# A hybrid decoder layer on one core: the key batches and the sample softmax moved between projection units, the memory pages turned one by one in one bank

## What is computed

```python
x = x + 0.5 * swiglu_ffn(x, ffn1_norm, ffn1_w_in, ffn1_w_out)
proj = rmsnorm(x, mix_norm) @ w_in          # u | q | k | v | q_mem, 256+512+512+512+256 columns
y_pool = pool_mixer(u, buf, ...)            # windows 2, 4, 8, 16, then 64x64 maps
q = rotary(rmsnorm(q)); k = rotary(rmsnorm(k))
y_moba = moba_attention(q, k_all, v_all)    # 8 heads; sample: 1024 cached keys in pages, best 3 of 4 blocks + own
y_mem = mem_attention(rmsnorm(qm), mk, mv)  # 4 heads into 256 memory tokens
x = x + concat(y_pool, y_moba, y_mem) @ w_out
x = x + 0.5 * swiglu_ffn(x, ffn2_norm, ffn2_w_in, ffn2_w_out)
```

## Time and profile before

| | us |
|---|---|
| three runs | 593.26, 593.95, 594.25 |
| median | 593.95 |
| the profiled execution | 594.11 |
| its span, first to last instruction | 592.3 |
| TensorE busy | 570.4 |
| VectorE busy | 394.4 |
| ScalarE busy | 264.4 |
| mean granted clock of TensorE | 0.993 |

### The profile page before, as it was taken

The page is one execution under the profiler, slowest core; times in us unless marked ns, Lnnn a source line. Parts: engine busy times, 40 slices in busy tenths (PEclk is TensorE's granted clock), DMA queues, the critical chain, the costliest instruction groups (busy, mean ns, idle before and its releaser), DMA issues.

```text
span 592.3 us, 13485 instructions
## 1 busy us (share of the span) xinstructions
PE 570.4 (96%) x5104; PEld 522.7 (88%) x5104; DVE 394.4 (67%) x707; ACT 264.4 (45%) x420; POOL 16.1 (3%) x24
## 2 busy tenths in 40 slices
PE   9999999999999999988899968999999999999997
PEld 7999999999899997655576746989999999999997
DVE  4776767768688876996654443488777776774443
ACT  5834345354543345433354654564343434353331
POOL 1000000000000003000000000040000000000000
PEclk9999999999999999998999989999999999999999
DMA  8799988775677638897999925446666666575522
GB/s 220 215 261 296 257 260 239 221 228 191 224 237 240 224 107 293 312 386 269 328 330 308 352 72 182 117 127 185 179 177 177 177 177 177 177 242 184 177 71 74
DMA packets 133121, 128.41 MB, mean 217 GB/s; under 512 B 6624, under 2 KB 103991, under 8 KB 133071
## 3 DMA queue, kind: packets, MB, share of 16 engines
q1 hardware_dynamic: 132791, 127.76, 68.5%
q10 hardware_dynamic: 288, 0.08, 0.1%
HBM read 125.12 MB, written 2.83 MB: 216 GB/s over the span
## 4 chain that ended last, share of the span: by engine, by line
PE 75%; DVE 11%; issue 5%; ACT 5%; DMA 2%; SPq 1%; DVEq 0%; ACTq 0%
PE banks L1451 21%; PE banks L1453 20%; PE banks L1452 20%; PE banks L1459 4%; DVE w_lo L976 3%; ACT w_hi L679 3%; PE banks L1860 2%; DVE kv L987 2%; PE banks L1590 2%; DMA raw<-in_w_in 1%; PE banks L1781 1%; PE banks L1560 1%; DVE h_tmp L1022 1%; DVE h_tmp L1017 1%; DVE sg L1012 1%
## 5 line engine op out<-in xcount | busy, mean ns | idle before, releaser
L976 DVE TENSOR_TENSOR w_lo<-raw,w_hi 128x1024 fp32r<-128x1024 f32 x158 | 193.3, 1230 | 107.7 <-ACT w_hi L679 106.3
L1451 PE MATMUL banks<-x_hi,w_hi 128*128 128x264 f32 x768 | 221.4, 288 | 2.5 <-DVE h_tmp L1017 0.9
L1452 PE MATMUL banks<-x_lo,w_hi 128*128 128x264 f32 x768 | 218.0, 284 | 0.0
L1453 PE MATMUL banks<-x_hi,w_lo 128*128 128x264 f32 x768 | 217.9, 284 | 0.0
L679 ACT ACTIVATE w_hi<-raw 128x1024 fp32r<-128x1024 f32 x158 | 161.8, 1050 | 89.3 <-PE banks L1453 76.0
L1451 PEld LDWEIGHTS banks<-x_hi,w_hi 128*128 128x128 f32 x768 | 145.0, 189 | 5.8 <-issue 2.2
L1452 PEld LDWEIGHTS banks<-x_lo,w_hi 128*128 128x128 f32 x768 | 145.2, 189 | 0.0
L1453 PEld LDWEIGHTS banks<-x_hi,w_lo 128*128 128x128 f32 x768 | 144.4, 188 | 0.0
L1451 PE MATMUL banks<-h_hi,w_hi 128*128 (+1 forms) x352 | 100.2, 285 | 0.0
L1453 PE MATMUL banks<-h_hi,w_lo 128*128 (+1 forms) x352 | 100.2, 285 | 0.0
L1452 PE MATMUL banks<-h_lo,w_hi 128*128 (+1 forms) x352 | 100.0, 284 | 0.0
(11 more groups left out here) (280 smaller groups left out, 505.4 us busy)
## 6 DMA issues: line engine op xcount, KB each, us to landing
raw<-in_ffn_w_in SPq DMA_DIRECT2D x86, 512.0 KB, 4.3
raw<-in_ffn_w_out SPq DMA_DIRECT2D x44, 512.0 KB, 3.4
kv<-in_cache_k SPq DMA_DIRECT2D x56, 256.0 KB, 4.8
kv<-in_cache_v SPq DMA_DIRECT2D x48, 256.0 KB, 5.0
raw<-in_w_in SPq DMA_DIRECT2D x12, 512.0 KB, 6.3
late_slot<-in_cache_v SPq DMA_DIRECT2D x16, 256.0 KB, 4.6
raw<-in_w_out SPq DMA_DIRECT2D x8, 512.0 KB, 5.8
raw<-in_mem_w_kv SPq DMA_DIRECT2D x4, 512.0 KB, 3.3
```

Source lines behind the costliest of these rows:

```text
L976: vec.tensor_tensor(w_lo[:, n % RING, :], raw[:, n % RING, :], w_hi[:, n % RING, :].bitcast(F32), ALU.subtract).then_inc(lo_ready, 1)
L1451: pe.matmul(out, lhs[0], rhs[0], start=start, stop=False)
L1452: pe.matmul(out, lhs[0], rhs[1], start=False, stop=False)
L1453: return pe.matmul(out, lhs[1], rhs[0], start=False, stop=stop)
```

## The change

- The table: sample projections 4 to 7 stand together ahead of unit 3's last piece; key batches 0 to 4 one piece later, batches 5, 6, 7 ahead of piece 2 of unit 5, piece 2 of unit 7 and piece 3 of unit 8 (before: 0 of 5, 1 of 6, 2 of 7). The softmax steps A0 to A5 move from units 8 to 10 to units 8 to 12, value batch 0 from the end of unit 10 into unit 12, all heads a unit or more later. Pages 0 to 3 are turned during unit 15, pages 4 to 7 in the tail between other steps, each alone.
- One bank (6) and one semaphore pair for all page turns. Page 0 waits until the outputs of heads 0 to 3 have left the bank, each further page until the one before has been copied back. The scores of the last two heads wait for all pages and for pooling's banks.
- The first unit of the second feed-forward makes the products with the high part of x first, waiting for that, and those with the low part behind.
- The last four projection units take their weight blocks in the order 1, 2, 3, 0 instead of 2, 3, 0, 1; SyncE reads the page numbers of batch 6 ahead of the memory keys and those of batch 7 behind value batch 5.

```diff
-HY_BANKS, POOL_BANKS, MK_BANKS, QM_BANK = (6, 3, 4), (4, 5), (6, 5, 4), 7
+HY_BANKS, POOL_BANKS, MK_BANK, QM_BANK = (6, 3, 4), (4, 5), 6, 7
...
-J_ORDER = (2, 3, 0, 1)
+J_ORDER = (2, 3, 0, 1) * 3 + (1, 2, 3, 0)
...
-            8: {0: [("OWN", 0), ("A", 0)], 1: [("OWN", 1)], 2: [("S", 10), ("NV", 4), ("ND", 4)], 3: [("A", 1)], 4: [("A", 2), ("S", 11), ("ES", 2)]},
-            9: {0: [("A", 3), ("WL", 11)], 2: [("NS", 4), ("NG", 4), ("A", 4)], 4: [("WL", 12)]},
...
+            8: {0: [("OWN", 0)], 2: [("NV", 4), ("ND", 4)], 3: [("K", 7)], 4: [("S", 10), ("A", 0), ("OWN", 1)]},
+            9: {0: [("WL", 11)], 1: [("A", 1)], 2: [("A", 2), ("S", 11), ("ES", 2)], 4: [("WL", 12)]},
...
+            keep_pages(6)
             load_memory("mk")
-            keep_pages(6)
+            load_batch("v", 5)
             keep_pages(7)
-            load_batch("v", 5)
...
-                act.wait_ge(k_turned[b % 3], b // 3 + 1)
-                act.activation(mem_page(b), bank[MK_BANKS[b % 3]][:, :], ACT.Copy).then_inc(kT_ready[b % 3], 1)
+                act.wait_ge(k_turned, b + 1)
+                act.activation(mem_page(b), bank[MK_BANK][:, :], ACT.Copy).then_inc(kT_ready, 1)
...
-                for idx, k in enumerate((range(KT), M_ORDER)[f]):
-                    if k_at is not None:
+                order = (range(KT), M_ORDER)[f]
+                if k_at is not None:
+                    w = lambda k: weights(n % RING, k * P, (k + 1) * P)
+                    out = bank[b0 + j][:, 0:N]
+                    for idx, k in enumerate(order):
+                        pe.wait_ge(xhi_ready, k_at + idx + 1)
+                        pe.matmul(out, w(k)[0], x_hi[:, k, :], start=(idx == 0), stop=False)
+                        pe.matmul(out, w(k)[1], x_hi[:, k, :], start=False, stop=False)
+                    for idx, k in enumerate(order):
                         pe.wait_ge(xlo_ready, k_at + idx + 1)
+                        mm = pe.matmul(out, w(k)[0], x_lo[:, k, :], start=False, stop=(idx == KT - 1))
...
                 if b == 0:
                     pe.wait_ge(hy_lo, 1)
-                elif b < 3:
-                    pe.wait_ge(pool_lo, 2)
                 else:
-                    pe.wait_ge(kT_ready[b % 3], b // 3)
+                    pe.wait_ge(kT_ready, b)
...
                     if k == 5:
-                        pe.wait_ge(kT_ready[0], mem_last(6))
-                        pe.wait_ge(kT_ready[1], mem_last(5))
+                        pe.wait_ge(kT_ready, NS)
+                        pe.wait_ge(pool_lo, 2)
```

More of the change, by code:

```diff
@@ L272, in layer @@
         s_stats, s_shared, s_sums = sem("s_stats"), sem("s_shared"), sem("s_sums")
-        k_turned, kT_ready = [sem(f"k_turned{i}") for i in range(3)], [sem(f"kT_ready{i}") for i in range(3)]
+        k_turned, kT_ready = sem("k_turned"), sem("kT_ready")
         q_turned, mk_used = sem("q_turned"), sem("mk_used")
@@ L346, in mem_page @@
             return slots[SLOT_OF["mk", 0]][:, b * 512:(b + 1) * 512]
-        def mem_last(bank_):
-            return len([b for b in range(NS) if MK_BANKS[b % 3] == bank_])
         def key_pair(g):
@@ L557, in load_projection @@
             def load_projection(r):
-                j = J_ORDER[r % 4]
+                j = J_ORDER[r]
                 if r < 12:
@@ L979, in key_evac @@
             def key_evac(b):
-                vec.wait_ge(k_turned[b % 3], b // 3 + 1)
-                vec.tensor_copy(mem_page(b), bank[MK_BANKS[b % 3]][:, :]).then_inc(kT_ready[b % 3], 1)
+                vec.wait_ge(k_turned, b + 1)
+                vec.tensor_copy(mem_page(b), bank[MK_BANK][:, :]).then_inc(kT_ready, 1)
             def turn_pair(g):
@@ L1464, in ffn_unit @@
                 pe.wait_ge(lo_ready, i * 4 + (n + 1))
-                for idx, k in enumerate((range(KT), M_ORDER)[f]):
-                    if k_at is not None:
+                order = (range(KT), M_ORDER)[f]
[7 more added lines that the diff above has]
+                    for idx, k in enumerate(order):
                         pe.wait_ge(xlo_ready, k_at + idx + 1)
+                        mm = pe.matmul(out, w(k)[0], x_lo[:, k, :], start=False, stop=(idx == KT - 1))
+                for idx, k in enumerate(order if k_at is None else ()):
                     mm = three(bank[b0 + j][:, 0:N], weights(n % RING, k * P, (k + 1) * P),
@@ L1559, in project_samples @@
                         c0 = kk * 512 + q * P
-                        mm = pe.matmul(bank[S_BANK][32 * q:32 * q + NS, 0:P], xs[:, 2 * J_ORDER[j] + kk, :], raw[:, n % RING, c0:c0 + P],
+                        mm = pe.matmul(bank[S_BANK][32 * q:32 * q + NS, 0:P], xs[:, 2 * J_ORDER[r] + kk, :], raw[:, n % RING, c0:c0 + P],
                                        start=(j + kk == 0), stop=(j + kk == 4))
@@ L1568, in key_turns @@
                     pe.wait_ge(hy_lo, 1)
-                elif b < 3:
-                    pe.wait_ge(pool_lo, 2)
                 else:
-                    pe.wait_ge(kT_ready[b % 3], b // 3)
+                    pe.wait_ge(kT_ready, b)
                 for c in range(4):
-                    mm = turn(bank[MK_BANKS[b % 3]][:, c * P:(c + 1) * P], mem_page(b)[:, c * P:(c + 1) * P])
-                mm.then_inc(k_turned[b % 3], 1)
+                    mm = turn(bank[MK_BANK][:, c * P:(c + 1) * P], mem_page(b)[:, c * P:(c + 1) * P])
+                mm.then_inc(k_turned, 1)
             def key_logits(b):
@@ L1597, in mem_key_logits @@
                 pe.wait_ge(qkT_ready, 6)
-                for side in range(3):
-                    pe.wait_ge(kT_ready[side], mem_last(MK_BANKS[side]))
+                pe.wait_ge(kT_ready, NS)
                 for b in range(4):
@@ L1801, in _ @@
                     elif k == 4:
[L1802 removed]
+                        pe.wait_ge(pool_lo, 1)
                     masked = k < MH // 2
@@ L1873, in _ @@
                 pe.wait_ge(res_ready, KT + j + 1)
-                ffn_unit(1, 0, j, 2 * KT)
+                ffn_unit(1, 0, j, None if j else 2 * KT)
             ffn_unit(1, 0, 2)
```

9 lines of the change are left out of this document (3 added, 6 removed), and 44 rows, old and new, of tables (EXTRA, TAIL).

## The result

The changed kernel takes 605.27 us (median of four runs, 602.87 to 606.01); the kernel before, beside it, 593.61. The ratio is 1.019, with a 95% interval of 1.016 to 1.022. The prediction said 602.1 with a range of 597 to 607. As a difference it said 8.2 us more than before; 11.7 were measured (the interval is 9.4 to 13.1), so the time lies in the range, but nearer to rival three (605.9) than to the forecast. The profiled execution took 605.17 us with a span of 603.4, 11.1 more than before.

A forecast was written before the change was run, and what follows sets the result against it. Bound: softmax steps on in-order ScalarE held behind weight splits waiting for SyncE's full queue. 7.4 - 8.7 + 3.6 + 1.7 + 3.4 + 0.5 = 7.9, plus 0.3, on 594.1, less 0.15: 602.1 us, range 597 to 607.

The forecast's parts named there:

- rival three: Slower still: two more half-clock stretches and the upper end of the queue's delay, 605.9 us; chance 0.16.
- unit 8's weights sent: SyncE's queue: this send waits for sample projection 4 and goes out at 244.5, 2.4 us later than before.
- unit 13's weights later by: SyncE's queue: these weights land 1.5 us later, ends 0.3 and 2.4, at 290.0.
- sum A4: Softmax sum on TensorE: exponentials held behind unit 13's weight split, so it comes at 294.0 after waiting 11.4 us.
- first piece of unit 12: TensorE waits another 3.5 us, until 300.35, for an evacuation behind ScalarE's split of unit 14's weights.
- idle time, unit 12 to the first output product: New TensorE waits: 3.6 us at page 0, 1.7 up to the tail and 3.4 in the tail.
- page 0 of it: Page 0's turn waits 3.6 us for the split of heads 0 to 3's outputs, behind heads 4 and 5's exponentials.
- half clock after unit 12: TensorE at half clock behind the new waits: 0.5 us taken, ends 0 and 3.4.
- The two holds: ScalarE's splits of units 13 and 14 wait for transfers, holding exponentials, then copy and evacuation: waits of 11.4 and 3.5 us.
- The tail: Five waits of 0.4, 0.6, 0.8, 0.9 and 0.7 us up to the first output product, 3.4 together, ends 1 and 6.
- Rival two: No change: 7.4 us lost, but the tail has no waits and 8.7 are won in full, 593.1 us; chance 0.04.
- Rival one: Faster: the exponentials are not held behind unit 13's weights, 587.4 us; chance 0.08.

The follow-up runs named there:

- e4: Kernel before, with only the softmax exponentials and sum moved later, behind ScalarE's split of unit 13's weights: 603.0 us, ratio 1.014.
- e7: Changed kernel with sample projections 4 and 5 back at the end of unit 2: 604.05 us, ratio 1.014.
- e2: Changed kernel with ScalarE's split of unit 13's weights moved behind the exponentials: 606.6 us, ratio 1.019.
- e9: Changed kernel with the splits of units 13 (both engines' halves), 14 and 15 moved later, behind steps TensorE waits for: 596.15 us, ratio 1.002.
- e12: e11 plus ScalarE's split of unit 16's weights moved behind the copy of page 0: 588.7 us, ratio 0.988 to the kernel before.
- e10: Changed kernel with the split of heads 0 to 3's outputs and the sample copy ahead of heads 4 and 5's maxima and exponentials: 603.7 us, ratio 1.016.
- e1: Changed kernel with ScalarE's split of unit 13 behind the exponentials and that of unit 14 behind the value projection's evacuations: 601.1 us, ratio 1.011.
- e3: Changed kernel with 34 products of ones by ones on TensorE ahead of its wait at the softmax sum: 606.3 us, ratio 1.019.
- e5: Changed kernel with ScalarE's splits of units 13 and 14 both behind the value projection's evacuations: 602.5 us, ratio 1.010.
- e6: e5 plus the split of heads 0 to 3's outputs ahead of heads 4 and 5's maxima and exponentials: 600.1 us, ratio 1.008.
- e11: Changed kernel with the moves of e9, e10 and e7 and the second feed-forward's first unit in its old order: 590.7 us, ratio 0.993.

## Why the prediction was right, step by step

The forecast named the mechanism and its places; what was off were sizes, and they partly cancel. That they cancel is luck.

| step | predicted | in the profile |
|---|---|---|
| unit 8's weights sent | 244.5 | 243.50 |
| wait of the last key batch | 0.5 | none |
| wait at A1 | 1.3 | 0.8 |
| TensorE reaches the sum | 282.6 | 280.8 (1.1 of it the earlier start) |
| unit 13's weights later by | 1.5 | 0.9 (2.0 without the earlier start) |
| sum A4 | 294.0, wait 11.4 | 293.56, wait 12.8 |
| first piece of unit 12 | 300.35, wait 3.5 | 299.24, wait 0.6 |
| idle time, unit 12 to the first output product | 8.7 | 8.0 |
| page 0 of it | 3.6 | 3.5 |
| half clock after unit 12 | 0.5 | 5.3 |
| first output product | 7.9 later | 10.2 later |
| first unit of the second feed-forward | 0.3 | 1.05 |

**Up to the softmax** TensorE came 1.8 us sooner than I had it. Of this 1.1 are the earlier start of the stretch in this profile, not the change; the rest is that the last key batch did not wait and A1 waited 0.8. The send of unit 8's weights, 1.0 earlier than forecast, is the same 1.1: counted from the query columns it is 2.5 us later than before, and 2.4 had been worked out. My reading that SyncE sends without a pause was too strong, though: in the kernel before nothing is sent from 259.4 to 263.9 and from 269.9 to 274.4. The time gained ahead of the sum was worth nothing, since the sum is tied to the landing of unit 13's weights. That is what e4 and e7 show: with quite different ways up to that point, the sum begins 4.1 us after that split begins.

**The two holds** are shown by e2 and e9. Their end, 299.24, was 1.1 us earlier than forecast, because unit 14's weights were only 0.4 later than before, not 1.5 (1.5 without the earlier start). On another chip they were over 2 later (split at 298.89 in e2). The term was right in kind, but its spread for unit 13, about 2 to 4.6 us without the shifts of the start, goes well past my upper end of 2.4.

**The step that was mis-sized is the clock.** I wrote that the stretch behind the long wait would be swallowed, and took 0.5 us for the rest. TensorE worked at half clock from 293.56 on; the second hold then had only 0.6 us of wait left to give, so the stretch ran 3.8 us into unit 12 and cost 1.9 there. Two more stretches of 3.4 us came, at page 0 and at the memory values, 1.7 each: 5.3 in all, 4.8 more than taken. With the 1.1 us of the hold and the 0.7 us of idle time on the other side, that makes 3 of more delay; the first output product shows 2.3, and the 0.7 between them stays unassigned. Counted from the query columns the product is 11.3 us later than before, 3.4 more than forecast.

**The tail** was near in its sum, 8.0 us for 8.7, and that is partly luck. Page 0's wait was right. Of the 1.7 us between page 0 and the end of unit 15 only 0.4 came, for the last evacuation; the waits of page 1 and of the transposes of heads 4 and 5 did not show in this profile, where TensorE's work there ran at half clock. The five waits of the tail were 0.3, 0.8, 1.0, 1.0 and 0.7, together 3.9 for 3.4, close each to what following two engines through the new order had given.

**The rivals.** Rival two, no change, fell with the 8.0 us of idle time that it had put at nothing. Rival one, 587.4, needed exponentials that are not held. e9 takes the hold of unit 13 away and does not reach it, 596.15: it keeps 3.7 us at the sum (behind the split of unit 12), 3.5 at page 0 and three half-clock stretches. e12, with more moves, gets to 588.7. Rival three, two more stretches at half clock and a later queue, had 605.9 and the measurement gives 605.27: of its two parts the stretches came in the profile; the queue was about 2 us late, between forecast and rival, and later than the rival in some of the other profiles. My likeliest case should have held at least one of these stretches, since the earlier trace rows showed one near waits of about 2 us.

## What to carry to other kernels

When a step is moved later on an in-order engine, list what it is moved past, and ask of each such instruction whether it waits for a transfer: a ready softmax behind a weight split costs what the transfer is late, however short the step. Removing such a hold shows the next one, on this engine or on the one that does the other half of the split, so move all halves of all the waiting splits behind the last step that TensorE needs, and read the time, not the wait that vanished. And where the trace of before already shows half clock behind such waits, put some of it into the sum for each new one.

## What was not expected of the hardware

The length of the half-clock stretch. Before the change two stretches lasted 3.4 us each. Behind the wait of 12.8 us it was 17 us (286.0 to 303.07), of which TensorE was idle 7.5 and then worked 9.5 with small gaps; e10 shows 286.4 to 300.0, e1 284.6 to 298.3 and e4 some 13.7 us from 285 on, each begun within the wait at the sum. And half clock did not follow each wait of the same length: the same 1.01 us wait ahead of the memory values was followed by half clock in the changed kernel, e1, e7 and e9 (3.4 to 3.6 us for the 64 products) and by full clock in e2, e3, e5, e6, e10, e11 and e12 (1.93 or 1.94 us). Five of these seven (e2, e3, e5, e6 and e11) had a stretch of 3.4 us in the first units of the second feed-forward instead; the four with half clock at the memory values had none there. What decides this the runs do not tell.
